# High parts of the gain-scaled transposed rows written by ScalarE instead of VectorE

## The chip, the cores and the metric

The kernel runs on one core of one Trainium2 chip. The metric is the device time of one execution in microseconds (us), the median of several. A profile of one further execution gives the trace that is read here. In views, PE is TensorE's matmul (PEld its weight load), ACT is ScalarE, DVE is VectorE, SP is SyncE, which issues nearly all DMAs.

## The reference

Two transformer blocks follow each other on 256 rows of width 2048, all in fp32. What matters here is that every block begins its stages with an RMS norm that has a weight vector `g`, and that the normed rows feed large matrix products:

```python
h = rmsnorm(x, g_mix)                       # 256 x 2048
proj = h @ w_in                             # then attention branches, gates
x = x + merged @ w_out
hm, mem_n = rmsnorm(x, g_mem_q), rmsnorm(mem, g_mem_kv)
x = x + mem_cross_attn(hm, mem_n, ...)
x = x + square(relu(rmsnorm(x, g_ff) @ w_ff1)) @ w_ff2
x = rmsnorm(x, g_final)                     # end of the first block
h = rms_norm(x, attn_norm);  x = x + hybrid_mixer(h, ...)
x = x + swiglu(rms_norm(x, ffn_norm), w_gate, w_up, w_down)
```

## The kernel before

A product of two fp32 matrices is done as three products of rounded parts (type fp32r): high x high, high x low, low x high. The weights come from HBM in groups of two k-tiles (128 x 1024 elements, 512 KB), through a ring of four buffers. For each group ScalarE writes the high part (`round_group`, L782) and VectorE the low part (`rest_to`, L1045); PE then runs 12 matmuls of 512 columns on it (L899 to L901), into two PSUM banks that belong to one 512-column chunk of the result.

The stationary side is the transposed rows, also in a high and a low part (`act_a_hi`, `act_a_lo`, `act_b_hi`, `act_b_lo`). A step "T" (a turn) makes two k-tiles of it: PE transposes four 128x128 blocks into one of the two auxiliary banks (L967) and raises `aux_done`; VectorE reads the bank and writes both parts (`turned`), and raises `aux_out`. The bank is free for the turn after the next, and the group that takes these tiles may start. Where the rows have still to be multiplied by a norm's weights (`"gain"` in the step), VectorE multiplies each half of the bank by a column of `gains` (L1241, two instructions of 256 columns) and then subtracts (L1245, two more). There are 50 such turns: 8 each for `g_mix`, `g_mem_kv`, `g_mem_q`, `g_ff`, `attn_norm_2` and `ffn_norm_2`, and 2 for `g_cq`. None of them is in a loop over repeated groups.

The order is written out by hand in `plan()`, as one list of steps; each engine walks the whole list and does its own part of each step, strictly in order. `weave` and `lead` put side steps between a chunk's groups. At step "G" number g, ScalarE rounds group g+3 (when its weights have landed and group g-1 is done) and VectorE does the low part of group g+2. Before the walk, ScalarE rounds the first three groups:

```python
for g in range(RING - 1):
    round_group(g, Turn())
```

The kernel then begins with `lead(cq, xt)`: turns 0 and 1, squares of the first rows (L838), group 0, turn 2, group 1, turn 3 and so on. SyncE loads weights and rows alternately: group 0, x part 0, group 1, x part 1, group 2, ... Before a group's load, SyncE waits until VectorE has done with the buffer (`lo_ready`).

Another place that is spoken of below is the start of the second block (around 1490 to 1550 us): there the steps "twice" (L1348, L1349) and "rstd" put much work on VectorE between the turns for `attn_norm_2`.

Of the kernel before, what the change touches and what calls it, by code (L numbers as in the profile page):

```python
# [32 lines left out]
ALU = mybir.AluOpType  # L33
ACT = mybir.ActivationFunctionType
AX = mybir.AxisListType

P = 128
SEQ = 256
# [39 lines left out]
G_ROWS = {"g_mix": 0, "g_mem_q": 16, "g_mem_kv": 32, "g_ff": 48, "attn_norm_2": 64, "ffn_norm_2": 80,  # L78
          "g_cq": 96, "fox_q_norm_2": 100, "fox_k_norm_2": 101, "nsa_q_norm_2": 102, "cmp_k_norm_2": 103,
          "slc_k_norm_2": 104, "win_k_norm_2": 105, "g_final": 106}  # L80
# [415 lines left out]
def two_blocks(nc, a, out):  # L496
    segments, groups = number(plan())
    ctx = ExitStack()
    with ctx:
# [3 lines left out]
        def sem(name):  # L503
            return ctx.enter_context(nc.semaphore(name))
# [22 lines left out]
        gains = sb("gains", [P, P])  # L527
# [56 lines left out]
        w_landed = [sem(f"w_landed{i}") for i in range(RING)]  # L584
        hi_ready, lo_ready, group_done = sem("hi_ready"), sem("lo_ready"), sem("group_done")
        chunk_out = [sem("chunk_out0"), sem("chunk_out1")]
        aux_done = sem("aux_done")
        aux_out = [sem("aux_out0"), sem("aux_out1")]
        rows_ready = sem("rows_ready")
        scores_done, row_max_ready, exp_done, probs_ready = map(sem, ("scores_done", "row_max_ready", "exp_done", "probs_ready"))  # L590
# [10 lines left out]
        def pt_of(unit, slot):  # L601

            return pt_sb[:, unit["u"] % 2 * 512:unit["u"] % 2 * 512 + 512] if unit["kind"] == "mem" else pt_sb[:, slot * 3 * P:(slot + 1) * 3 * P]

        def weights(c, i, turn):

# [158 lines left out]
        @block.scalar  # L765
        def _(act_e):
            act_e.dma_start(g_rows[0:KT, :], a["g_mix"].rearrange("a (k p) -> (a k) p", p=P)).then_inc(gmix_landed, 16)
            n, rstds, xs, sums = [0], [0], [0], [0]

            def step(ins):  # L770
                ins.then_inc(act_step, 1)
                n[0] += 1
                act_e.wait_ge(act_step, n[0])

            def round_group(g, turn):

                s, w = g % RING, groups[g]["width"]
                wait(act_e, w_landed[s], groups[g]["landed"], turn.landed)
                if g >= RING:

                    wait(act_e, group_done, g - RING + 1, turn.g)
                nc.scalar.activation(whi[:, s, 0:w], raw[:, s, 0:w], ACT.Copy).then_inc(hi_ready, 1)  # L782

            for g in range(RING - 1):
                round_group(g, Turn())

            def leave(c, turn):
                ev = c["ev"]
                if ev not in ("gate", "silu"):
                    return  # L790
                wait(act_e, group_done, c["end"], turn.g)
                wait(act_e, rstd_ready, rstds[0])
                if ev == "silu" and c["c"] >= 2:

                    wait(act_e, chunk_out[(c["c"] + 1) % 2], (c["c"] + 1) // 2, turn.c2)
                for t in range(NT):
                    src = prod_bank[c["c"] % 2 * 2 + t][:, :]
                    if ev == "gate":
                        ins = nc.scalar.activation(val[c["to"]][:, t, c["off"]:c["off"] + CH], src, ACT.Tanh, scale=s_("half_h", t, t + 1))
                    else:  # L800
                        ins = nc.scalar.activation(stage[:, 0, t, :], src, ACT.Silu, scale=s_("rstd_h", t, t + 1))
                ins.then_inc(chunk_out[c["c"] % 2], 1)

            def visit(kind, what, turn):
                if kind == "G":
                    if what["g"] + RING - 1 < len(groups):
                        round_group(what["g"] + RING - 1, turn)
                elif kind == "E":
                    leave(what, turn)
                elif kind == "gates":  # L810


                    act_e.wait_ge(forget_in, 1)
                    step(nc.scalar.activation(s_("e16"), s_("e16"), ACT.Exp, scale=-1.0))
                    nc.scalar.activation(s_("e16"), s_("e16"), ACT.Ln, bias=1.0).then_inc(forget_act, 1)
                    nc.scalar.activation(s_("gate"), s_("gate"), ACT.Tanh, scale=0.5).then_inc(gate_act, 1)
                elif kind == "rope":
                    act_e.wait_ge(angle_ready, 1)
                    nc.scalar.activation(s_("sin_in"), s_("sin_in"), ACT.Sin)
                    nc.scalar.activation(s_("red"), s_("red"), ACT.Sin).then_inc(sine_ready, 1)  # L820
                elif kind == "rstd":
                    rstds[0] += 1
                elif kind == "Q":
                    m = what["m"]
                    if what["of"] == "mem":
                        act_e.wait_ge(mem_landed, 16 * NT)
                    elif "r_fixed" in what["rows"]:
                        act_e.wait_ge(x_landed[m], 16)
                    else:
                        act_e.wait_ge(chunk_out[what["rows_c"] % 2], what["rows_c"] // 2 + 1)  # L830
                    if rstds[0]:

                        act_e.wait_ge(rstd_ready, rstds[0])
                    if sums[0]:

                        act_e.wait_ge(squared, sums[0])
                    for t in range(NT):
                        ins = nc.scalar.activation(act_junk[:, :], val[what["of"]][:, t, m * CH:(m + 1) * CH], ACT.Square,  # L838
                                                   accum_out=s_("ss", 4 * t + m, 4 * t + m + 1))
                        if t == 0:  # L840
                            step(ins)
                    ins.then_inc(squared, 1)
                    sums[0] += 1
                elif kind == "X":
                    x, j = xs[0], what["j"]
                    xs[0] += 1
                    act_e.wait_ge(aux_done, j + 1)
                    if x >= 2:
                        act_e.wait_ge(scored, x - 1)
                    nc.scalar.activation(rel[:, x % 2, :], aux_bank[j % 2][:, :], ACT.Relu).then_inc(aux_out[j % 2], 1)  # L850
                elif kind == "S":
                    u = what["u"]
                    act_e.wait_ge(row_max_ready, u + 1)
                    for t, (lo, hi) in enumerate(spans(what)):
                        v = s_sb[:, u % 2, lo:hi]
                        src = s_bank[u % 2][:, lo:hi] if what["kind"] == "mem" else v
                        total = None if what["kind"] == "cmp" else s_("rsum", u % 2 * 2 + t, u % 2 * 2 + t + 1)
                        ins = nc.scalar.activation(v, src, ACT.Exp, bias=s_("nmax", u % 2 * 2 + t, u % 2 * 2 + t + 1), scale=1.0, accum_out=total)  # L858
                    ins.then_inc(exp_done, 1)

            walk(act_e, visit, "act")


# [152 lines left out]

        @block.vector
        def _(dve):
            n, base, xs, rests, seen = [0], [0], [0], [0], [-1]
            v_e = nc.vector  # L1020

            def step(ins):

                ins.then_inc(dve_step, 1)
                n[0] += 1
                dve.wait_ge(dve_step, base[0] + n[0])
# [200 lines left out]
            def turned(what, turn):  # L1227
# [3 lines left out]
                if what["to"] in "AB":  # L1231
                    hi, lo = act[what["to"]]
                    cols = slice(k * SEQ, (k + 2) * SEQ)
                    if "gain" not in what:
                        step(v_e.tensor_copy(hi[:, cols], b[:, :]))  # L1235
                        v_e.tensor_tensor(lo[:, cols], b[:, :], hi[:, cols].bitcast(F32), ALU.subtract).then_inc(done, 1)
                        return
                    g0 = G_ROWS[what["gain"]] + (what["gain_k"] + what["col"] // P if "gain_k" in what else k)
                    for kk in range(2):
                        c1 = slice((k + kk) * SEQ, (k + kk + 1) * SEQ)  # L1240
                        ins = v_e.tensor_scalar(hi[:, c1], b[:, kk * SEQ:(kk + 1) * SEQ], gains[:, g0 + kk:g0 + kk + 1], None, ALU.mult)  # L1241
                    step(ins)
                    for kk in range(2):
                        c1 = slice((k + kk) * SEQ, (k + kk + 1) * SEQ)
                        ins = v_e.scalar_tensor_tensor(lo[:, c1], b[:, kk * SEQ:(kk + 1) * SEQ], gains[:, g0 + kk:g0 + kk + 1],  # L1245
                                                       hi[:, c1].bitcast(F32), ALU.mult, ALU.subtract)
                    ins.then_inc(done, 1)
                    return
# [260 lines left out]
```

## Time and profile before

| | us |
|---|---|
| median of 3 runs | 2705.02 (2704.07 to 2705.16) |
| the profiled execution | 2701.03 |
| its span, first to last instruction | 2699.3 |
| PE busy | 2657.9 (98%) |
| VectorE busy | 1785.9 (66%) |
| ScalarE busy | 1072.2 (40%) |

The span leaves 1.7 us of the profiled execution outside. A busy share is an average over stages. PE's share is modelled from pipelined matmuls; what PE isn't busy, 41.4 us, is the sum of its visible waits. The profiled execution lies 4 us below the median of the others, so differences are worked out against the trace and then added to the median.

### The profile page before, as it was taken

The page shows a single profiled execution, that of the slowest core. Times are in us where ns is not written, and L with a number is a line of the kernel's source. Part 1 is how long each engine was busy: PE and PEld are TensorE (multiplying, and loading weights), DVE is VectorE, ACT ScalarE, POOL GpSimd, SP SyncE. Part 2 cuts the span into 40 slices and gives each one's busy share as a digit, 9 for nine tenths or more (in the row PEclk, how much of TensorE's full clock was granted, in tenths as well). Part 3 has the DMA queues.
Part 4 walks back from the last instruction along what each step waited for, and adds up shares of the span by engine and source line. Part 5 has one row for each costly group of instructions (what it writes and reads, how often), then busy time and mean ns, then how long its engine had stood idle before and what let it go on. Part 6 is the DMA issues. An engine that isn't in the chain of part 4 may idle for free.

```text
span 2699.3 us, 33835 instructions
## 1 busy us (share of the span) xinstructions
PE 2657.9 (98%) x12280; PEld 2204.4 (82%) x12280; DVE 1785.9 (66%) x2651; ACT 1072.2 (40%) x1269; POOL 7.9 (0%) x43
## 2 busy tenths in 40 slices
PE   8999999999999999999999998999999999999998
PEld 7978888888878888888888777887888888888887
DVE  7678775576776656655665878898755555555555
ACT  4333344534343333333333433433343343444342
POOL 0000000000000000000000000000000000000000
PEclk9999999999999999999999998999999999999999
DMA  6545556555545555555555455444465555555554
GB/s 220 182 156 165 155 164 218 194 181 189 173 146 188 188 199 180 187 194 186 193 187 202 156 172 163 145 140 133 147 198 188 186 187 193 191 191 192 188 191 159
DMA packets 262080, 483.60 MB, mean 179 GB/s; under 512 B 17706, under 2 KB 38372, under 8 KB 261604
## 3 DMA queue, kind: packets, MB, share of 16 engines
q1 hardware_dynamic: 261956, 482.37, 54.6%
q8 instruction: 58, 0.95, 0.1%
q14 instruction: 34, 0.28, 0.0%
q10 hardware_dynamic: 32, 0.01, 0.0%
HBM read 480.22 MB, written 2.10 MB: 179 GB/s over the span
## 4 chain that ended last, share of the span: by engine, by line
PE 93%; DVE 5%; DMA 1%; issue 1%; ACT 0%; DVEq 0%; SPq 0%; ACTq 0%
PE bank L899 29%; PE bank L901 29%; PE bank L900 29%; PE bank L967 2%; DVE w_split L1045 2%; PE bank L930 1%; PE bank L998 1%; PE bank L983 1%; PE bank L1000 0%; PE bank L977 0%; DMA w_raw<-in_cmp_w_v 0%; PE bank L935 0%; DVE stage L1130 0%; DVE small L1072 0%; DVE scratch L1071 0%
## 5 line engine op out<-in xcount | busy, mean ns | idle before, releaser
L782 ACT ACTIVATE w_split<-w_raw 128x1024 fp32r<-128x1024 f32 (+2 forms) x920 | 959.9, 1046 | 1373.3 <-PE bank L901 1308.2
L1045 DVE TENSOR_TENSOR w_split<-w_raw,w_split 128x1024 fp32r<-128x1024 f32 (+2 forms) x920 | 1084.0, 1202 | 224.4 <-ACT w_split L782 221.9
L899 PE MATMUL bank<-w_split,act_a_hi 128*128 128x512 f32 (+2 forms) x2400 | 947.2, 395 | 10.1 <-DVE w_split L1045 9.1
L901 PE MATMUL bank<-w_split,act_a_lo 128*128 128x512 f32 (+2 forms) x2400 | 927.2, 386 | 0.0
L900 PE MATMUL bank<-w_split,act_a_hi 128*128 128x512 f32 (+2 forms) x2400 | 925.8, 386 | 0.0
L899 PEld LDWEIGHTS bank<-w_split,act_a_hi 128*128 128x128 f32 x2400 | 453.5, 189 | 97.6 <-DVE w_split L1045 7.1
L901 PEld LDWEIGHTS bank<-w_split,act_a_lo 128*128 128x128 f32 x2400 | 452.7, 189 | 89.2
L900 PEld LDWEIGHTS bank<-w_split,act_a_hi 128*128 128x128 f32 x2400 | 453.8, 189 | 82.9
L899 PE MATMUL bank<-w_split,act_b_hi 128*128 128x512 f32 x1248 | 490.8, 393 | 3.2 <-issue 2.9
L901 PE MATMUL bank<-w_split,act_b_lo 128*128 128x512 f32 x1248 | 486.3, 390 | 0.0
L900 PE MATMUL bank<-w_split,act_b_hi 128*128 128x512 f32 x1248 | 485.9, 389 | 0.0
L899 PEld LDWEIGHTS bank<-w_split,act_b_hi 128*128 128x128 f32 x1248 | 234.4, 188 | 53.5 <-issue 5.9
L901 PEld LDWEIGHTS bank<-w_split,act_b_lo 128*128 128x128 f32 x1248 | 234.2, 188 | 49.5
L900 PEld LDWEIGHTS bank<-w_split,act_b_hi 128*128 128x128 f32 x1248 | 234.5, 188 | 47.3
L1188 DVE TENSOR_TENSOR xres<-bank,xres 128x512 f32<-128x512 f32 x184 | 118.4, 685 | 185.6 <-PE bank L901 185.6
L1235 DVE CAST act_b_hi<-bank 128x512 fp32r<-128x512 f32 x54 | 37.3, 691 | 161.4 <-PE bank L967 161.4
L858 ACT ACTIVATE s_sb<-s_sb,small 128x128 f32<-128x128 f32 (+1 forms) x96 | 40.5, 431 | 169.6 <-DVE small L1288 169.6
L967 PE MATMUL bank<-ident,stage 128*128 128x128 f32 x386 | 57.7, 275 | 7.4 <-DVE stage L1078 6.9
L967 PEld LDWEIGHTS bank<-ident,stage 128*128 128x128 f32 x386 | 47.7, 141 | 19.5 <-issue 8.9
L1241 DVE TENSOR_SCALAR act_a_hi<-bank,gains 128x256 fp32r<-128x256 f32 x80 | 35.0, 478 | 27.2 <-PE bank L967 27.1
L1192 DVE TENSOR_SCALAR stage<-bank,small 128x512 f32<-128x512 f32 x32 | 22.5, 746 | 36.2 <-PE bank L901 36.2
L930 PE MATMUL bank<-heads 128*128 128x128 f32 (+2 forms) x208 | 43.2, 325 | 0.4 <-issue 0.4
(181 smaller groups left out, 926.0 us busy)
## 6 DMA issues: line engine op xcount, KB each, us to landing
w_raw<-in_w_ff SPq DMA_DIRECT2D x256, 512.0 KB, 4.4
w_raw<-in_w_in SPq DMA_DIRECT2D x208, 512.0 KB, 3.6
w_raw<-in_w_gate SPq DMA_DIRECT2D x88, 512.0 KB, 4.3
w_raw<-in_w_up SPq DMA_DIRECT2D x88, 512.0 KB, 4.6
w_raw<-in_w_down SPq DMA_DIRECT2D x88, 512.0 KB, 4.6
w_raw<-in_w_out SPq DMA_DIRECT2D x64, 512.0 KB, 4.0
w_raw<-in_w_in SPq DMA_DIRECT2D x24, 368.0 KB, 3.6
w_raw<-in_w_dsa_o SPq DMA_DIRECT2D x16, 512.0 KB, 4.8
```

Of the source, the lines that this page charges most:

```text
L782: nc.scalar.activation(whi[:, s, 0:w], raw[:, s, 0:w], ACT.Copy).then_inc(hi_ready, 1)
L858: ins = nc.scalar.activation(v, src, ACT.Exp, bias=s_("nmax", u % 2 * 2 + t, u % 2 * 2 + t + 1), scale=1.0, accum_out=total)
L899: pe.matmul(o, hi[:, cols], rhs_hi, start=k == 0, stop=False)
L900: pe.matmul(o, hi[:, cols], rhs_lo, start=False, stop=False)
L901: ins = pe.matmul(o, lo[:, cols], rhs_hi, start=False, stop=k == c["kt"] - 1)
L930: ins = pe.matmul(o, q[:, t * P:(t + 1) * P], k[:, 0:hi - lo], start=True, stop=not fox)
L967: ins = pe.transpose(b[:, kk * SEQ + t * P:kk * SEQ + (t + 1) * P], src[:, t, what["col"] + kk * P:what["col"] + (kk + 1) * P], ident[:, :])
L983: ins = pe.transpose(b[0:hi - lo, to:to + P], v[:, lo:hi], ident[:, :])
L1045: v_e.tensor_tensor(wlo[:, s, 0:w], raw[:, s, 0:w], whi[:, s, 0:w].bitcast(F32), ALU.subtract).then_inc(lo_ready, 1)
L1188: ins = v_e.tensor_tensor(x, b[t], x, ALU.add)
L1235: step(v_e.tensor_copy(hi[:, cols], b[:, :]))
L1241: ins = v_e.tensor_scalar(hi[:, c1], b[:, kk * SEQ:(kk + 1) * SEQ], gains[:, g0 + kk:g0 + kk + 1], None, ALU.mult)
```

## The change

ScalarE's walk now has a part for turns with a gain: it waits for the transposes (`aux_done`), multiplies both halves of the bank by their columns of `gains` into the high part, and raises a new semaphore, `turned_hi`. VectorE waits for that semaphore instead of multiplying, and then does only the subtraction. The first such step on ScalarE also waits until the first `gains` are written. Turns without a gain are as they were.

```diff
@@ -584,7 +584,7 @@
         w_landed = [sem(f"w_landed{i}") for i in range(RING)]
         hi_ready, lo_ready, group_done = sem("hi_ready"), sem("lo_ready"), sem("group_done")
         chunk_out = [sem("chunk_out0"), sem("chunk_out1")]
-        aux_done = sem("aux_done")
+        aux_done, turned_hi = sem("aux_done"), sem("turned_hi")
         aux_out = [sem("aux_out0"), sem("aux_out1")]
         rows_ready = sem("rows_ready")
         scores_done, row_max_ready, exp_done, probs_ready = map(sem, ("scores_done", "row_max_ready", "exp_done", "probs_ready"))
@@ -601,6 +601,9 @@
         def pt_of(unit, slot):
 
             return pt_sb[:, unit["u"] % 2 * 512:unit["u"] % 2 * 512 + 512] if unit["kind"] == "mem" else pt_sb[:, slot * 3 * P:(slot + 1) * 3 * P]
+
+        def gain_row(what):
+            return G_ROWS[what["gain"]] + (what["gain_k"] + what["col"] // P if "gain_k" in what else what["k"])
 
         def weights(c, i, turn):
 
@@ -765,7 +768,7 @@
         @block.scalar
         def _(act_e):
             act_e.dma_start(g_rows[0:KT, :], a["g_mix"].rearrange("a (k p) -> (a k) p", p=P)).then_inc(gmix_landed, 16)
-            n, rstds, xs, sums = [0], [0], [0], [0]
+            n, rstds, xs, sums, turns_hi = [0], [0], [0], [0], [0]
 
             def step(ins):
                 ins.then_inc(act_step, 1)
@@ -841,6 +844,17 @@
                             step(ins)
                     ins.then_inc(squared, 1)
                     sums[0] += 1
+                elif kind == "T" and "gain" in what:
+                    j, k = what["j"], what["k"]
+                    act_e.wait_ge(aux_done, j + 1)
+                    if turns_hi[0] == 0:
+                        act_e.wait_ge(aux_out[0], 1)
+                    for kk in range(2):
+                        g0 = gain_row(what) + kk
+                        ins = nc.scalar.activation(act[what["to"]][0][:, (k + kk) * SEQ:(k + kk + 1) * SEQ], aux_bank[j % 2][:, kk * SEQ:(kk + 1) * SEQ],
+                                                   ACT.Copy, scale=gains[:, g0:g0 + 1])
+                    ins.then_inc(turned_hi, 1)
+                    turns_hi[0] += 1
                 elif kind == "X":
                     x, j = xs[0], what["j"]
                     xs[0] += 1
@@ -1016,7 +1030,7 @@
 
         @block.vector
         def _(dve):
-            n, base, xs, rests, seen = [0], [0], [0], [0], [-1]
+            n, base, xs, rests, seen, turns_hi = [0], [0], [0], [0], [-1], [0]
             v_e = nc.vector
 
             def step(ins):
@@ -1235,11 +1249,9 @@
                         step(v_e.tensor_copy(hi[:, cols], b[:, :]))
                         v_e.tensor_tensor(lo[:, cols], b[:, :], hi[:, cols].bitcast(F32), ALU.subtract).then_inc(done, 1)
                         return
-                    g0 = G_ROWS[what["gain"]] + (what["gain_k"] + what["col"] // P if "gain_k" in what else k)
-                    for kk in range(2):
-                        c1 = slice((k + kk) * SEQ, (k + kk + 1) * SEQ)
-                        ins = v_e.tensor_scalar(hi[:, c1], b[:, kk * SEQ:(kk + 1) * SEQ], gains[:, g0 + kk:g0 + kk + 1], None, ALU.mult)
-                    step(ins)
+                    g0 = gain_row(what)
+                    turns_hi[0] += 1
+                    dve.wait_ge(turned_hi, turns_hi[0])
                     for kk in range(2):
                         c1 = slice((k + kk) * SEQ, (k + kk + 1) * SEQ)
                         ins = v_e.scalar_tensor_tensor(lo[:, c1], b[:, kk * SEQ:(kk + 1) * SEQ], gains[:, g0 + kk:g0 + kk + 1],
```

Line numbers move: L782 of before is L785 after, L838 is L841, L1045 is L1059, L1245 is L1257; the new multiplication is L854. PE's and SyncE's instructions keep their order.

What ScalarE's queue holds at the start of the kernel, before (w_split<-w_raw is the rounding of a weight group, act_junk the squares):

```order
L782 ACTIVATE w_split<-w_raw 128x1024 x3
L838 ACTIVATE act_junk,small<-xres 128x512 x2
L782 ACTIVATE w_split<-w_raw 128x1024 x2
L838 ACTIVATE act_junk,small<-xres 128x512 x2
L782 ACTIVATE w_split<-w_raw 128x1024 x2
```

and after:

```order
L785 ACTIVATE w_split<-w_raw 128x1024 x3
L854 ACTIVATE act_a_hi<-bank,gains 128x256 x4
L841 ACTIVATE act_junk,small<-xres 128x512 x2
L785 ACTIVATE w_split<-w_raw 128x1024
L854 ACTIVATE act_a_hi<-bank,gains 128x256 x2
L785 ACTIVATE w_split<-w_raw 128x1024
L854 ACTIVATE act_a_hi<-bank,gains 128x256 x2
```

The high parts of turns 0 and 1 now stand behind the roundings of the first three weight groups.

VectorE's queue at the same place, before:

```order
L1357 COPY gains<-bank 128x16
L1045 TENSOR_TENSOR w_split<-w_raw,w_split 128x1024
L1241 TENSOR_SCALAR act_a_hi<-bank,gains 128x256 x2
L1245 SCALAR_TENSOR_TENSOR act_a_lo<-bank,gains,act_a_hi 128x256 x2
L1241 TENSOR_SCALAR act_a_hi<-bank,gains 128x256 x2
L1245 SCALAR_TENSOR_TENSOR act_a_lo<-bank,gains,act_a_hi 128x256 x2
L1045 TENSOR_TENSOR w_split<-w_raw,w_split 128x1024
```

and after:

```order
L1369 COPY gains<-bank 128x16
L1059 TENSOR_TENSOR w_split<-w_raw,w_split 128x1024
L1257 SCALAR_TENSOR_TENSOR act_a_lo<-bank,gains,act_a_hi 128x256 x4
L1059 TENSOR_TENSOR w_split<-w_raw,w_split 128x1024
```

The two pairs of L1241 are gone and nothing else has moved, but the first L1257 now waits for ScalarE.

ScalarE's queue at the start of the second block, after; the four pairs of L854 are turns 4 to 7 for `attn_norm_2`. Before, the same rows stand there without L854:

```order
L785 ACTIVATE w_split<-w_raw 128x1024 x2
L854 ACTIVATE act_a_hi<-bank,gains 128x256 x2
L785 ACTIVATE w_split<-w_raw 128x1024 x2
L841 ACTIVATE act_junk,small<-xres 128x512 x2
L854 ACTIVATE act_a_hi<-bank,gains 128x256 x2
L785 ACTIVATE w_split<-w_raw 128x1024 x2
L854 ACTIVATE act_a_hi<-bank,gains 128x256 x2
L785 ACTIVATE w_split<-w_raw 128x1024 x2
L854 ACTIVATE act_a_hi<-bank,gains 128x256 x2
```

Each pair stands ahead of the rounding that follows its turn.

## Rows read from the trace of the kernel before

**Rows 1.** Busy time by stretch: us, PE, PEld, DVE, ACT, POOL, granted clock, DMA.

```profile
1480.00:1560.00 80.00, 74.62 (x342) 60.23 (x341) 69.78 (x140) 32.79 (x42) 2.85 (x12) 1.00 0.50 161
```

**Rows 2.** Waits: who <- whom, us in total, times, longest.

```profile
DVE act_a_hi L1241 <- PE bank L967: 27.1, 29, 3.5
DVE act_b_hi L1241 <- PE bank L967: 24.2, 10, 3.5
PE bank L899 <- DVE w_split L1045: 9.1, 8, 2.0
```

**Rows 3.** Groups by shape: busy us, mean ns of one, idle before.

```profile
L1241 DVE TENSOR_SCALAR act_a_hi<-bank,gains 128x256 fp32r<-128x256 f32 x80 | 35.0, 478 | 27.2 <-PE bank L967 27.1
L858 ACT ACTIVATE s_sb<-bank,small 128x256 f32<-128x256 f32 x8 | 3.7, 472 | 9.6 <-DVE small L1288 9.6
L799 ACT ACTIVATE heads<-bank,small 128x512 f32<-128x512 f32 x16 | 10.1, 684 | 13.9 <-PE bank L901 13.9
```

**Rows 4.** Order of time, start: start us, us, engine; merged when a count follows.

```profile
4.88 1.06 ACT L782 ACTIVATE w_split<-w_raw 128x1024 fp32r<-128x1024 f32 x1 [2.29 <-DMA w_raw<-in_w_in]
6.05 1.23 DVE L1045 TENSOR_TENSOR w_split<-w_raw,w_split 128x1024 fp32r<-128x1024 f32 x1 [1.58 <-ACT w_split L782]
8.04 0.88 DVE L1241 TENSOR_SCALAR act_a_hi<-bank,gains 128x256 fp32r<-128x256 f32 x2 [0.76 <-PE bank L967]
8.95 0.87 DVE L1245 SCALAR_TENSOR_TENSOR act_a_lo<-bank,gains,act_a_hi 128x256 fp32r<-128x256 f32 x2
9.88 0.80 PE L899 MATMUL bank<-w_split,act_a_hi 128*128 128x512 f32 x1 [1.02 <-DVE act_a_lo L1245]
11.10 1.06 ACT L782 ACTIVATE w_split<-w_raw 128x1024 fp32r<-128x1024 f32 x1 [1.65 <-DMA w_raw<-in_w_in]
12.06 0.62 ACT L838 ACTIVATE act_junk<-xres 128x512 f32<-128x512 f32 x1
15.90 0.88 DVE L1241 TENSOR_SCALAR act_a_hi<-bank,gains 128x256 fp32r<-128x256 f32 x2 [3.25 <-PE bank L967]
17.61 2.35 DVE L1045 TENSOR_TENSOR w_split<-w_raw,w_split 128x1024 fp32r<-128x1024 f32 x2
```

**Rows 5.** The chain that ended last, start: start us, us, what.

```profile
10.67 0.43 PE bank L900
...
15.37 0.50 PE bank L967 x4
15.86 0.23 PE bank L899
...
18.64 0.44 PE bank L967 x4
```

**Rows 6.** Order of time: PE, then ScalarE behind it; and a ScalarE pair of 512 columns.

```profile
217.09 1.13 PE L977 MATMUL bank<-misc,heads 64*128 64x256 f32 x4
...
218.25 0.60 ACT L850 ACTIVATE s_sb<-bank 128x512 f32<-128x512 f32 x1 [3.57 <-PE bank L977]
...
370.15 1.27 ACT L799 ACTIVATE heads<-bank,small 128x512 f32<-128x512 f32 x2 [2.63 <-PE bank L901]
```

**Rows 7.** Order of time, start of the second block: VectorE, then PE.

```profile
1512.35 0.87 DVE L1241 TENSOR_SCALAR act_a_hi<-bank,gains 128x256 fp32r<-128x256 f32 x2 [1.67 <-PE bank L967]
...
1518.16 2.35 DVE L1045 TENSOR_TENSOR w_split<-w_raw,w_split 128x1024 fp32r<-128x1024 f32 x2
...
1531.66 0.87 DVE L1241 TENSOR_SCALAR act_a_hi<-bank,gains 128x256 fp32r<-128x256 f32 x2 [0.30 <-PE bank L967]
...
1519.53 0.47 PE L899 MATMUL bank<-w_split,act_a_hi 128*128 128x512 f32 x1 [1.29 <-DVE w_split L1045]
...
1537.65 0.47 PE L899 MATMUL bank<-w_split,act_a_hi 128*128 128x512 f32 x1 [0.55 <-DVE w_split L1045]
1548.07 0.50 PE L899 MATMUL bank<-w_split,act_a_hi 128*128 128x512 f32 x1 [2.02 <-DVE w_split L1045]
```

## The prediction

> **What bounds the kernel now.** I read the busy times first, in the table above: PE is busy 2657.9 of 2699.3 us, VectorE for 66%, ScalarE for 40%. So of the whole span only 41.4 us are PE's waits, and time taken off VectorE is worth something only where PE stands still because VectorE is late. Next I asked for waits by name. VectorE's low parts of the weights hold PE up for 9.1 us in 8 places [rows 2]. Three of these 8 lie between 1480 and 1560 us, where PE is busy for 74.62 of 80 us and VectorE for 69.78 [rows 1]: 1.29, 0.55 and 2.02 us, at 1519.53, 1537.65 and 1548.07 [rows 7]. This is the only place where turns with a gain and PE's waits for VectorE lie together, and it holds 3.86 us.
>
> The same view says how the turns stand: before the multiplication VectorE had been idle, waiting for PE's transposes, in 29 + 10 = 39 of the 50 turns [rows 2]. There the turn is no backlog but a chain: transposes, high part, low part. In the other 11 VectorE came late, and only these can start their low part earlier when the high part moves away.
>
> Last I read the start in order of time. PE's first group waits for the low part of turn 0: multiplication at 8.04, subtraction at 8.95, first matmul at 9.88 [rows 4]. ScalarE rounds three weight groups there, as they land: the first at 4.88, the third not before 11.10, since its DMA ends then.
>
> **Removed.** 100 multiplications on VectorE at 478 ns [rows 3], two to a turn; a pair takes from 8.04 to 8.95, 0.91 us, until the subtraction starts [rows 4]. The 50 pairs are some 44 us of VectorE's 1786.
>
> **Added.** 100 multiplications on ScalarE, 256 columns out of PSUM with a column of numbers as scale. The trace has no such instruction, but it has near ones: 256 columns out of PSUM with a column as bias take 472 ns, and 512 columns out of PSUM with a column as scale 684 ns [rows 3]. A pair of the latter takes 1.27 us, so two overlap by 2 x 0.684 - 1.27 = 0.10 us [rows 6]. I take 2 x 0.472 - 0.10 = 0.84 us for a pair. It can't cost more than the pair of 512 columns, 1.27; the lower bound is one instruction alone, 0.47. ScalarE starts behind PE as quickly as VectorE does: 217.09 + 1.13 = 218.22, start at 218.25 [rows 6]. VectorE starts behind ScalarE 0.11 us later: 4.88 + 1.06 = 5.94, start at 6.05 [rows 4]. So where the transposes release the turn, the low part starts after 0.84 + 0.11 = 0.95 us instead of 0.91: +0.04 us. The turn gets no shorter; it only runs on two engines.
>
> The Trainium skill, ScalarE: Activation LUTs, section What ACT_TABLE_LOAD costs, gives 186 ns plus 0.833 ns a column, about 93 ns for each column operand, and 93 ns of overlap; an estimate from it is 2 x 492 - 93 = 891 ns for the pair. Its section Rules for kernel authors would leave multiplications on VectorE for speed; the rows here, 478 against 472 ns, show no such advantage for fp32 out of PSUM.
>
> **The start: the term that decides.** ScalarE walks in order, and the high part of turn 0 stands behind the rounding of the third weight group. After that rounding ScalarE took its next instruction at 12.06 [rows 4]; that slot now goes to turn 0. Its pair ends at 12.06 + 0.84 = 12.90, VectorE starts the low part at 13.01 and ends 0.87 later at 13.88, and PE starts 0.06 behind it, as 8.95 + 0.87 = 9.82 and 9.88 before: at 13.94. That is 13.94 - 9.88 = **+4.06 us**. Nothing of it hides: PE has nothing else to do there, it is busy without a gap from 9.88 on, and the waits later on are gated by PE and VectorE one behind the other, not by a fixed time. What VectorE does next shifts too: the low part of group 1 follows turn 1 and frees its buffer some 4 us later, so later loads start later by about what their consumers do. Turn 1's high part follows directly on ScalarE and is done before VectorE wants it.
>
> Then turn 2 is checked. Before, it starts at 15.90, and the low part of the weights of PE's third group, the first of the two at 17.61, ends at 17.61 + 1.18 = 18.8 [rows 4]; PE's transposes ahead of that group end at 18.64 + 0.44 = 19.1 [rows 5]. The 0.3 us between them cover the added 0.04, but not much more.
>
> **PE's pace.** The first group's matmuls of 512 columns follow each other every 0.43 us, from 9.88 to 15.37 [rows 4, 5], which is the 1.2 GHz level; afterwards every 0.23 us, and the second group takes 18.64 - 15.86 = 2.78 us [rows 5]. Before its first matmul PE had run transposes and then waited 1.0 us; now that wait is 5.1 us. If the slow stretch moves along unchanged the cost is 0. If the first group ran fast throughout, 5.49 - 2.78 = 2.7 us come back; if one more group runs slowly, 2.7 more are lost. I take 0 and keep both ends.
>
> **The second block's start.** VectorE's work without a pause before 1519.53 begins with turn 4, which the transposes release at 1512.35; that before 1537.65 and 1548.07 begins with turn 7, released at 1531.66 [rows 7]. Both turns are of the kind that gets 0.04 longer, so the three waits stay: 2 x 0.04 = +0.08 us. Turns 5 and 6 between them are late ones; their low parts start about 0.9 and 1.7 us earlier (one and two pairs of 0.87), and VectorE then waits for the transposes of turn 7 that much longer. ScalarE's roundings behind each turn start some 1.2 us later (transposes and pair), but they are for a group that PE reaches three groups, over 8 us, later, so PE doesn't see it. The other turns stand in stages in which PE doesn't wait for VectorE at all.
>
> **Sum.** 4.06 + 0.08 = +4.1 us: against the trace 2701.03 + 4.1 = 2705.2 with a span of 2703.4; on the median of the runs, 2705.02 + 4.14 = **2709.2 us**, 0.15% slower. About 0.2% (5.4 us) is what a measurement of this kernel tells from no change, so this most likely counts as none.
>
> **Rivals.**
> - *VectorE's relief reaches PE* (0.10). The 3.86 us of waits at the second block's start go away, because the late turns 5 and 6 pull all behind them forward. For it: VectorE is the busiest there relative to its time. Against it: VectorE idles again before turn 7 [rows 7]. It would give 4.06 - 3.86 = +0.2, 2705.3 us, not slower.
> - *All of VectorE's relief counts* (0.03). The 11 late turns give back 0.87 us each, 9.6 us, and the time is 2709.1 - 9.6 = 2699.5. Against it: that is more than the waits of PE that lie near them.
> - *A ScalarE pair is dearer than taken* (0.17). With the upper bound of 1.27 us, each released turn is 0.43 longer. Turn 0 pays it, turn 2 beyond its 0.3, turns 4 and 7 in full: 0.43 + 0.13 + 0.86 = +1.4 on top of the forecast, so 2710.6 us, slower than the bound. It decides from a pair of about 1.2 us on.
> - *The start isn't late* (0.03): the third weight group lands before the rows do in other executions, and ScalarE is free at 8. It would give 2705.1. Against it: SyncE issues that load behind the first rows.
>
> The forecast has 0.67 left. The estimate from the skill's page would put 0.05 on each of three turns, 2709.3 us.
>
> **Range.** The forecast with the pace term's ends is 2706.5 to 2711.9; the relief rival adds 2705.3 below, the dear pair lies inside. I give 2705.2 to 2712.0. Slower by over 0.2% means above 2710.4: the dear pair and a tenth of the forecast, where PE's pace loses over 1.2 us: 0.17 + 0.07 = 0.24; faster 0.03; the rest 0.73.
>
> **What would show it.** In the changed profile the first L899 should start at 13.9, released by the low part of turn 0, and the first L854 at 12.06. L854 should be about 470 ns. PE's waits for the low parts of the weights between 1480 and 1560 should still be near 3.9 us, all shifted by 4. VectorE should be busy 44 us less and ScalarE some 42 to 47 more, with VectorE's waits "for PE's transposes" turned into waits for ScalarE. I am wrong if PE starts before 12, or if PE waits at one of the other turns for a bank or a high part: then ScalarE's queue holds something up that I took for free.

## The result, and the profile after

| us | before | after |
|---|---|---|
| median, side by side on one chip | 2702.72 (20 runs) | 2706.84 (20 runs) |
| the profiled execution | 2701.03 | 2705.11 |
| its span | 2699.3 | 2703.4 |
| VectorE busy | 1785.9 | 1743.6 |
| ScalarE busy | 1072.2 | 1108.2 |

The ratio is 1.0015 with an interval of [1.0009, 1.0021]: 4.1 us slower, 0.15%, inside the bound under which it counts as no change, but a real loss: the interval excludes 1. The prediction was +4.1 us, 0.15%. As a time it was 2709.2, which is 2.4 us too high, because it was added to a median of three executions (2705.02), and the median of twenty is 2702.72. Of all executions on record two lie far off the others, one of before beside experiments 1 to 4 (4469.2 us, mean clock 0.556) and one of experiment 2 (3327.21 us, 0.753), and neither is in a ratio below.

The busy times at the head of the page, after:

```profile
PE 2657.8 (98%) x12280; PEld 2204.4 (82%) x12280; DVE 1743.6 (64%) x2551; ACT 1108.2 (41%) x1369; POOL 7.9 (0%) x43
```

PE is busy for the same time to 0.1 us while the span is 4.1 us longer: all of the loss is PE waiting. VectorE works 42.3 us less, and nothing of that reaches the end.

The start in order of time, after (start us, us, engine; merged where a count follows; idle before and releaser in brackets), to be read against [rows 4]:

```profile
11.16 1.06 ACT L785 ACTIVATE w_split<-w_raw 128x1024 fp32r<-128x1024 f32 x1 [1.64 <-DMA w_raw<-in_w_in]
12.13 1.55 ACT L854 ACTIVATE act_a_hi<-bank,gains 128x256 fp32r<-128x256 f32 x4
13.06 1.66 DVE L1257 SCALAR_TENSOR_TENSOR act_a_lo<-bank,gains,act_a_hi 128x256 fp32r<-128x256 f32 x4 [5.89 <-ACT act_a_hi L854]
13.99 0.79 PE L913 MATMUL bank<-w_split,act_a_hi 128*128 128x512 f32 x1 [4.85 <-DVE act_a_lo L1257]
...
20.05 0.84 ACT L854 ACTIVATE act_a_hi<-bank,gains 128x256 fp32r<-128x256 f32 x2 [4.06 <-PE bank L981]
```

Read it from below: PE's first group starts at 13.99 instead of 9.88, released by the low part; that starts at 13.06, released by ScalarE; ScalarE has no idle time before 12.13, where L854 follows directly on the third rounding, and that rounding waited 1.64 us for its weights. So a transfer which turn 0 doesn't need now stands ahead of it.

The chain that ended last, after, start of the kernel (start us, us, what), against [rows 5]:

```profile
14.78 0.43 PE bank L914
...
19.05 0.43 PE bank L915
19.47 0.54 PE bank L981 x4
20.02 0.23 PE bank L913
```

The first group runs at the slow pace from 13.99 to 19.47, 5.48 us; before from 9.88 to 15.37, 5.49 us. The slow stretch moved along whole.

The new instructions, and VectorE's, grouped by shape (count, busy us, mean ns of one, idle before), against [rows 3]:

```profile
L854 ACT ACTIVATE act_a_hi<-bank,gains 128x256 fp32r<-128x256 f32 x80 | 33.4, 471 | 46.7 <-PE bank L981 46.6
L1257 DVE SCALAR_TENSOR_TENSOR act_a_lo<-bank,gains,act_a_hi 128x256 fp32r<-128x256 f32 x80 | 34.9, 479 | 67.4 <-ACT act_a_hi L854 67.1
```

Waits after (who <- whom: us in total, times, longest), against [rows 2]:

```profile
DVE act_a_lo L1257 <- ACT act_a_hi L854: 67.1, 35, 5.9
DVE act_b_lo L1257 <- ACT act_b_hi L854: 33.4, 10, 4.5
PE bank L913 <- DVE w_split L1059: 9.2, 8, 2.0
PE bank L913 <- DVE act_a_lo L1257: 4.8, 1, 4.8
```

This is where the 42 us went. Before, VectorE idled 51.3 us ahead of 39 turns; now 100.5 us ahead of 45. What was taken off its work came back as waiting in the same chain, transposes, high part, low part. Most of it is nothing but ScalarE's time: 0.95 us from the transposes to the low part, 50 times, would be 47.5 us (an estimate from the prediction's 0.84 + 0.11). PE's waits for the weights' low parts are 9.2 us in 8 places against 9.1 in 8, untouched. What has grown is one wait, that at the start: 4.8 us where it was 1.0 [rows 4].

The second block's start (busy by stretch, columns as in [rows 1], its window moved on by 4 us), and then its turns 4 and 7 and PE's waits in order of time, against [rows 7]:

```profile
1484.00:1564.00 80.00, 74.53 (x341) 60.22 (x340) 62.76 (x124) 38.01 (x58) 3.03 (x13) 1.00 0.51 161
```

```profile
1516.64 0.84 ACT L854 ACTIVATE act_a_hi<-bank,gains 128x256 fp32r<-128x256 f32 x2 [2.04 <-PE bank L981]
1517.58 0.88 DVE L1257 SCALAR_TENSOR_TENSOR act_a_lo<-bank,gains,act_a_hi 128x256 fp32r<-128x256 f32 x2 [2.77 <-ACT act_a_hi L854]
1523.86 0.47 PE L913 MATMUL bank<-w_split,act_a_hi 128*128 128x512 f32 x1 [1.32 <-DVE w_split L1059]
1536.90 0.88 DVE L1257 SCALAR_TENSOR_TENSOR act_a_lo<-bank,gains,act_a_hi 128x256 fp32r<-128x256 f32 x2 [2.76 <-ACT act_a_hi L854]
1541.97 0.47 PE L913 MATMUL bank<-w_split,act_a_hi 128*128 128x512 f32 x1 [0.58 <-DVE w_split L1059]
1552.40 0.50 PE L913 MATMUL bank<-w_split,act_a_hi 128*128 128x512 f32 x1 [1.99 <-DVE w_split L1059]
```

VectorE is busy 62.76 instead of 69.78 of 80 us, and PE 74.53 instead of 74.62. Ahead of turn 7 VectorE idles 2.76 us, before 0.30 [rows 7]. Of the 2.46 us more, some 0.9 are ScalarE's pair, which now stands between the transposes and the low part; the other 1.5 are what VectorE gained at the late turns 5 and 6, and all of it is spent waiting for the transposes of turn 7. PE's three waits are 1.32, 0.58 and 1.99 against 1.29, 0.55 and 2.02.

### The profile page after: what moved, and what is told of

Its sections match the earlier page's. It is cut to its first block, busy times and chain, and to the rows that moved or that the text cites. A ratio compares the mean times of both kernels' runs of the same rounds, so it can differ in the third digit from the quotient of the medians.

```text
span 2703.4 us, 33885 instructions
## 1 busy us (share of the span) xinstructions
PE 2657.8 (98%) x12280; PEld 2204.4 (82%) x12280; DVE 1743.6 (64%) x2551; ACT 1108.2 (41%) x1369; POOL 7.9 (0%) x43
## 4 chain that ended last, share of the span: by engine, by line
PE 92%; DVE 6%; DMA 1%; issue 1%; ACT 0%; SPq 0%; DVEq 0%; ACTq 0%
PE bank L913 29%; PE bank L915 29%; PE bank L914 29%; PE bank L981 2%; DVE w_split L1059 2%; PE bank L944 1%; PE bank L1012 1%; PE bank L997 1%; PE bank L1014 0%; PE bank L991 0%; DMA w_raw<-in_cmp_w_v 0%; DMA w_raw<-in_w_in 0%; PE bank L949 0%; DVE stage L1144 0%; DVE small L1086 0%
## 5 line engine op out<-in xcount | busy, mean ns | idle before, releaser
L785 ACT ACTIVATE w_split<-w_raw 128x1024 fp32r<-128x1024 f32 (+2 forms) x920 | 959.7, 1046 | 1275.7 <-PE bank L915 1215.1
L1059 DVE TENSOR_TENSOR w_split<-w_raw,w_split 128x1024 fp32r<-128x1024 f32 (+2 forms) x920 | 1084.6, 1203 | 224.5 <-ACT w_split L785 222.0
L1257 DVE SCALAR_TENSOR_TENSOR act_a_lo<-bank,gains,act_a_hi 128x256 fp32r<-128x256 f32 x80 | 34.9, 479 | 67.4 <-ACT act_a_hi L854 67.1
L854 ACT ACTIVATE act_a_hi<-bank,gains 128x256 fp32r<-128x256 f32 x80 | 33.4, 471 | 46.7 <-PE bank L981 46.6
```

Of the source, the lines that this page charges most:

```text
L854: ins = nc.scalar.activation(act[what["to"]][0][:, (k + kk) * SEQ:(k + kk + 1) * SEQ], aux_bank[j % 2][:, kk * SEQ:(kk + 1) * SEQ], ACT.Co ...
L1059: v_e.tensor_tensor(wlo[:, s, 0:w], raw[:, s, 0:w], whi[:, s, 0:w].bitcast(F32), ALU.subtract).then_inc(lo_ready, 1)
```

## The experiments

Single executions of one and the same kernel differ by up to 4 us either way of their median (the last section shows where), so a difference of 1 to 4 us is read in two ways below: by the medians with their interval, and by a milestone, the start of the first transposes for the block that follows the eight `attn_norm_2` turns. In the traces of before, after and the experiments it moves by what happened ahead of it, and not by the scatter behind it. The ratios and intervals below are not exactly the quotients of the medians beside them (0.9988 in experiment 7, where the medians give 0.9980); where the two differ, the interval is what counts. The milestone:

```profile
1558.56 0.60 PE L967 MATMUL bank<-ident,stage 128*128 128x128 f32 x4
```

is before, and after it is 4.35 us later:

```profile
1562.91 0.60 PE L981 MATMUL bank<-ident,stage 128*128 128x128 f32 x4
```

The theory: the loss is ScalarE's order at the start and nothing else, and the 42 us taken off VectorE are worth nothing as the order stands. Rivals: the loss is spread over 50 turns, each of them dearer; or the relief does give something and the start costs more than it seems.

### 1 and 2: the first two turns apart from the other 48

In the first kernel turns 0 and 1 keep the multiplication on VectorE, and 48 turns are changed; in the second only turns 0 and 1 are changed. The condition of the first:

```diff
-                elif kind == "T" and "gain" in what:
+                elif kind == "T" and "gain" in what and (not (what["gain"] == "g_mix" and what["k"] < 4)):
...
-                    turns_hi[0] += 1
-                    dve.wait_ge(turned_hi, turns_hi[0])
+                    if not (what["gain"] == "g_mix" and what["k"] < 4):
+                        turns_hi[0] += 1
+                        dve.wait_ge(turned_hi, turns_hi[0])
+                    else:
+                        for kk in range(2):
+                            c1 = slice((k + kk) * SEQ, (k + kk + 1) * SEQ)
+                            ins = v_e.tensor_scalar(hi[:, c1], b[:, kk * SEQ:(kk + 1) * SEQ], gains[:, g0 + kk:g0 + kk + 1], None, ALU.mult)
+                        step(ins)
```

The second has the same without the "not".

> The changed kernel, but turns 0 and 1 keep their multiplication on VectorE; the other 48 are on ScalarE. Theory (the whole loss is the start: turn 0 stands behind ScalarE's third rounding): the first matmul comes back from 13.99 to about 9.9 us, the span from 2703.4 to 2699.4, equal to the kernel before, within 0.3 us. Rival (the 48 later turns hold something up too, or give something back): the span differs from 2699.3 by over 0.5 us; if VectorE's relief reached PE at the second block's start it would be down to about 2695.5.

Measured: 2701.28 against 2702.24 of before, ratio 1.0000 [0.9991, 1.0009]. The first matmul starts at 9.97, the milestone is at 1558.87, +0.31 on before:

```profile
1558.87 0.60 PE L981 MATMUL bank<-ident,stage 128*128 128x128 f32 x4
```

The expectation had named the span, and its one profiled span is 2702.8, which by the expectation's own sign speaks for the rival. Matching each matmul of PE with the same one of before settles it: the kernel is 0.2 to 0.4 us later up to the milestone, loses 1.6 us between the milestone and 1710, most of it from 1682 to 1686, and 1.6 more between 1861 and 1866, with PE at a slower pace both times (last section), and nothing lasting elsewhere. The milestone isn't wholly free of that either: between 1548 and 1552 eight matmuls ran at 0.43 us and cost 1.5 us, and PE's waits behind them shrank by nearly as much (4.2 us in 4 places instead of 5.4 in 5 from 1475 to 1570), so that nothing of it is left at the milestone.

> Only turns 0 and 1 are multiplied on ScalarE; the other 48 stay on VectorE as before. Theory: the whole loss is there, first matmul at 14.0, span 2703.3. Rival (the loss is spread over the turns): the span stays near 2699.5.

Measured: 2704.91 against 2702.24 of before, ratio 1.0015 [1.0006, 1.0024], the ratio of the whole change. The chain that ended last, start of this kernel:

```profile
12.66 0.37 ACT act_a_hi L854
...
13.13 0.89 DVE act_a_lo L1263 x2
...
14.06 0.80 PE bank L913
...
17.42 0.43 PE bank L914
17.85 0.28 PE bank L915
18.12 0.23 PE bank L913
```

PE starts at 14.06, 4.18 later than before, and the milestone is only +3.40:

```profile
1561.96 0.60 PE L981 MATMUL bank<-ident,stage 128*128 128x128 f32 x4
```

The difference is here: PE goes over to the 0.23 us pace at 17.85, after 8 matmuls at the slow one instead of 12. So 4 of the 100 moved multiplications, those of turns 0 and 1, carry the whole loss, the 96 others carry none, and the length of the slow stretch is worth 0.8 us between this execution and the others.

### 3 and 4: the same 50 turns on ScalarE, but fewer roundings ahead of turn 0

If it is the order, then an order in which turn 0 stands ahead of the third rounding must give the loss back, with all the work still on ScalarE. Two of the three first roundings stay ahead in the third kernel, one in the fourth; the rest follows turn 1:

```diff
-            for g in range(RING - 1):
+            for g in range(1):
...
                     turns_hi[0] += 1
+                    if turns_hi[0] == 2:
+                        for g in range(1, RING - 1):
+                            round_group(g, Turn())
```

(with 2 for 1 in both places in the third).

> The changed kernel, but ScalarE takes turns 0 and 1 behind the second rounding instead of the third. Theory: turn 0's high part starts 0.97 us after the second rounding's start at 8.4, at 9.4, the first matmul 1.88 later at 11.25, so the span is 2700.7. If the loss came of anything else than the place in ScalarE's queue (a slower hand-over, PE's pace after the longer wait), the span doesn't follow the place: 2703.

Measured: 2703.46 against 2702.24, ratio 1.0007 [0.9998, 1.0016]; milestone 1559.82, +1.26. The expectation had named a span of 2700.7, and 2703 if the span didn't follow the place; the profiled span is 2703.6. The start and the milestone follow the place, and the 3.1 us behind the milestone are lost at the same two places as in experiment 1 (last section). PE's first group:

```profile
11.25 0.79 PE L916 MATMUL bank<-w_split,act_a_hi 128*128 128x512 f32 x1 [2.29 <-DVE act_a_lo L1260]
```

> As the last, but only the first rounding stands ahead of turns 0 and 1; all 50 turns on ScalarE. Theory: turn 0 is released by PE's transposes at 8.0 again, first matmul 9.92, span 2699.4, the time of the kernel before. Rival: the second and third roundings, now 1 to 2 us later, hold up PE's second or third group or the loads behind them, and the span is 2700.5 or more.

Measured: 2702.16 against 2702.24, profiled span 2699.8 (2699.4 expected), ratio 1.0006 [0.9997, 1.0015]; milestone 1558.89, +0.33.

```profile
10.00 0.80 PE L916 MATMUL bank<-w_split,act_a_hi 128*128 128x512 f32 x1 [1.06 <-DVE act_a_lo L1260]
```

Three roundings ahead, two, one: PE starts at 13.99, 11.25, 10.00, and the milestone is 4.35, 1.26 and 0.33 us later than before. The size of the loss follows the number of roundings ahead of the turn. The fourth kernel's waits for the weights between 1475 and 1570 are the same as in before, 5.4 us in 5 places, so even with the start mended the relief gives nothing.

### 5: every pair of multiplications done twice

This asks what cover the turns have for a dearer pair. Each high part is written twice, with a wait for the first writing between (the value is the same):

```diff
-                    for kk in range(2):
-                        g0 = gain_row(what) + kk
+                    for again in range(2):
+                        if again:
+                            step(ins)
+                        for kk in range(2):
+                            g0 = gain_row(what) + kk
...
```

> The changed kernel with every high part written twice on ScalarE, the second pair behind the first: each turn on ScalarE takes about 0.9 us more, 45 us of ScalarE in all. Theory (only the chains that PE waits for count: turn 0 at the start, turn 2 beyond its 0.3 us of cover, turns 4 and 7 at the second block's start): first matmul at 14.9, and the span 0.9 + 0.6 + 0.9 + 0.9 = 3.3 us above the changed kernel's 2703.4, 2706.7. Rival 1 (every turn that the transposes release counts, 39 x 0.9): 2738. Rival 2 (ScalarE's share of the work doesn't matter beyond the start): 2704.3.

Measured: 2713.32 against 2702.91 of before, ratio 1.0041 [1.0028, 1.0055]; the profiled span is 2710.8, 7.4 over the changed kernel's, where the theory expected 3.3. The start was as expected, PE at 14.83. PE's waits for the low parts of the weights, first over the kernel, then from 790 to 840, where the turns for `g_ff` lie:

```profile
PE bank L916 <- DVE w_split L1062: 11.9, 12, 2.2
```

```profile
PE bank L916 <- DVE w_split L1062: 1.1, 2, 1.0
```

That is 11.9 us in 12 places instead of 9.2 in 8, and PE didn't wait from 790 to 840 in before. The second block's start in order of time:

```profile
1529.36 0.47 PE L916 MATMUL bank<-w_split,act_a_hi 128*128 128x512 f32 x1 [2.20 <-DVE w_split L1062]
...
1548.35 0.47 PE L916 MATMUL bank<-w_split,act_a_hi 128*128 128x512 f32 x1 [1.13 <-DVE w_split L1062]
```

These waits were 1.32 and 0.58 after, so turns 4 and 7 pay 0.9 and 0.55 in them. Where the 7.4 us lie shows when the same matmul is looked up in both traces (start in us; both have the same 12280 matmuls in the same order):

| the same matmul | after | experiment 5 | later by |
|---|---|---|---|
| the first | 13.99 | 14.83 | 0.8 |
| behind turn 2 | 23.15 | 24.66 | 1.5 |
| behind turn 6 | 35.97 | 37.96 | 2.0 |
| in the turns for `g_mem_q` | 706.93 | 708.95 | 2.0 |
| behind them | 727.60 | 730.31 | 2.7 |
| at the end of the turns for `g_ff` | 829.45 | 833.98 | 4.5 |
| ahead of turn 4's wait, second block | 1519.21 | 1523.84 | 4.6 |
| the milestone | 1562.91 | 1569.24 | 6.3 |
| the end of the span | 2703.4 | 2710.8 | 7.4 |

The expectation had four turns and 3.3 us. Turn 0 is 0.8 us, turn 2 is 0.7, turns 4 and 7 together are 1.7, so these came out as expected. It failed on the sum: it took them as the only turns without cover, and 3.1 us more were lost ahead of the milestone, 0.5 behind turn 6 at the start, 0.7 behind the turns for `g_mem_q`, 1.8 at those for `g_ff` and 0.1 on the way to the second block. The last 1.1 us lie behind the milestone, where executions of one kernel scatter too. So most other turns are covered against a second pair, and a few only in part. The rival that all released turns pay (39 times 0.9, 35 us) is far off.

### 6 and 7: an order in which the relief can count

If the relief is worth nothing only because VectorE waits for turn 7's transposes, then long VectorE work put ahead of the turns instead of behind them should let it count. "twice" piece 1 stood behind turn 4 and piece 3 behind turn 7; now each stands ahead:

```diff
-    seq += weave(down[3], [squares(1, down[1]), xt[2], squares(2, down[2]), xt[3]] + distances[4:6] + [xt[4], twice[1]], 1)
-    pend = [squares(3, down[3])] + [xt[5], distances[6], twice[2], xt[6], distances[7], xt[7], twice[3]]
+    seq += weave(down[3], [squares(1, down[1]), xt[2], squares(2, down[2]), xt[3]] + distances[4:6] + [twice[1], xt[4]], 1)
+    pend = [squares(3, down[3])] + [xt[5], distances[6], twice[2], xt[6], distances[7], twice[3], xt[7]]
```

The sixth kernel is the fourth with this order; the seventh is before with this order and nothing else.

> One rounding ahead of turns 0 and 1 as in the run before, all turns on ScalarE, and in the order of steps at the second block's start the two pieces of 'twice' now stand before turns 4 and 7 instead of behind them. Theory: the multiplication moved to ScalarE left VectorE idle for 2.8 us before each of these turns, and 'twice' (2.9 us) now fills it; PE's waits for low parts between 1480 and 1560 fall from 5.4 to about 1.6 us, span 2699.8 - 3.8 = 2696.0. Rival (VectorE is bound by its work there, wherever the idle time lies): the waits only move, 5 us of them stay, span 2699.4.

Measured: 2697.10 against 2702.91, ratio 0.9978 [0.9969, 0.9987], 5.8 us faster than before. The milestone, and PE's waits for the weights from 1475 to 1570:

```profile
1554.40 0.60 PE L984 MATMUL bank<-ident,stage 128*128 128x128 f32 x4
```

```profile
PE bank L916 <- DVE w_split L1062: 1.6, 2, 1.0
```

The milestone is 4.16 us earlier than in before, and 5.4 us of waits have become 1.6.

> The kernel before, with the same two pieces of 'twice' ahead of turns 4 and 7. VectorE's idle time before these turns is 1.67 and 0.30 us here, since it multiplies itself. Theory: about 1.5 us of PE's waits between 1480 and 1560 go, 3.9 stay, span 2699.3 - 1.5 = 2697.8; the difference to the kernel with the multiplication on ScalarE, 1.8 us or more, is what VectorE's relief is worth there once the order lets it through. Rival (the relief is worth nothing there): both reordered kernels have the same waits within 0.3 us.

Measured: 2697.38 against 2702.91, ratio 0.9988 [0.9979, 0.9997]. Its milestone and the waits of the same stretch:

```profile
1556.29 0.60 PE L967 MATMUL bank<-ident,stage 128*128 128x128 f32 x4
```

```profile
PE bank L899 <- DVE w_split L1045: 2.0, 3, 1.0
PE bank L899 <- DVE act_a_lo L1245: 1.5, 1, 1.5
```

The order alone gives 2.27 us at the milestone, with 3.5 us of waits left. The new one of them, 1.5 us, is for a turn's low part, VectorE being late with its own multiplication: just what the change takes off it. With the turns on ScalarE that wait is gone, and 1554.40 against 1556.29, 1.9 us, is what VectorE's relief is worth at the milestone once the order lets it through.

At the end it isn't shown. The medians are 0.3 us apart, the intervals overlap, and both profiled spans are 2695.2 us. The two traces, sixth kernel first, still have the 1.9 us at the next wait, and lose 1.5 of them within 5 us behind it:

```profile
1594.97 0.63 PE L984 MATMUL bank<-ident,stage 128*128 128x128 f32 x4 [3.12 <-DVE stage L1095]
1596.86 0.63 PE L967 MATMUL bank<-ident,stage 128*128 128x128 f32 x4 [3.12 <-DVE stage L1078]
```

```profile
1590.00:1605.00 15.00, 11.88 (x48) 9.40 (x47) 11.22 (x23) 3.46 (x4) 0.00 (x0) 0.89 0.54 159
1590.00:1605.00 15.00, 11.88 (x55) 9.61 (x54) 12.73 (x26) 4.24 (x4) 0.00 (x0) 1.00 0.63 188
```

In the sixth kernel PE goes back to 0.43 us a matmul behind this wait of 3.12 us, at a granted clock of 0.89, as in before (0.89 there too); in the seventh it doesn't. The same transposes at 1679.32 and 1679.19 have nothing of the lead left. Why the seventh kept its clock stays open, and so does what the relief is worth at the end.

### 8: only the eight turns that can count

Only the turns for `attn_norm_2` on ScalarE, with the order of the sixth; the start is that of before.

```diff
-                elif kind == "T" and "gain" in what:
+                elif kind == "T" and "gain" in what and (what["gain"] == "attn_norm_2"):
```

> The reordered start of the second block ('twice' ahead of turns 4 and 7), but only the eight turns for attn_norm_2 have their high part on ScalarE; the other 42, those at the kernel's start among them, stay on VectorE. Theory (VectorE's relief is worth something only at this one place): the same as with all 50 turns moved and one rounding ahead, PE's waits for low parts between 1480 and 1560 at 1.6 us, span 2695.2 within 1 us. Rival (relief in the other 42 turns is worth something too): the span is above 2697, and PE's waits elsewhere are longer.

Measured: 2697.16 against 2702.63, ratio 0.9983 [0.9974, 0.9992]; 1.5 us of waits in 2 places between 1475 and 1570, and the milestone

```profile
1554.18 0.60 PE L981 MATMUL bank<-ident,stage 128*128 128x128 f32 x4
```

0.2 us from the sixth kernel's, and the profiled span is 2694.9 where 2695.2 was expected. Eight turns do all that fifty do, as far as these runs tell, and the start needs no mending.

Not tried: handing over half a bank at a time, VectorE subtracting the first half while ScalarE multiplies the second. It would have two engines read one bank at once.

## Why the prediction was right, point by point

**The start, +4.06.** Right in mechanism and size: L854 at 12.13 (12.06 foretold), PE at 13.99 (13.94), +4.11. That the whole time came out at +4.1 to a tenth is partly luck: the interval runs from 2.4 to 5.7 us, the milestone is 4.35 later, and 0.3 us of that is given back behind it. As an absolute time, 2706.84 lies nearer to the 2705.3 of the rival in which the relief reaches PE than to 2709.2; what speaks against that rival is the difference, and the waits that are still there. Experiments 1 and 2 show that turns 0 and 1 alone carry the loss; 3 and 4 that the roundings ahead of them are its cause.

**The pair, 0.84 us.** Right: 471 ns for one, 0.84 for the pair, from near rows of other shapes. The rival of a dearer pair is out. It was priced on the turns 0, 2, 4 and 7 alone; experiment 5, with some 0.9 us more for each turn, lost 3.0 us at other turns too, so the price was probably low, but a pair of 1.27 us was not run. The estimate from the Trainium skill, ScalarE: Activation LUTs, section What ACT_TABLE_LOAD costs, was 492 ns for one and 891 ns for the pair; the trace is about 20 and 50 ns lower.

**The second block, +0.08.** The three waits named are 3.89 us after against 3.86 before [rows 7]; two steps of 0.04 can't be told apart from that. The milestone, 4.35 later where the start is 4.11 later, leaves 0.24 us for everything between, a little more than foretold.

**A count that was wrong.** The prediction said that three waits lie between 1480 and 1560, 3.86 us. The view of waits for that stretch of before has five, two more behind the three:

```profile
PE bank L899 <- DVE w_split L1045: 5.4, 5, 2.0
```

The reading in order of time had stopped at 1548, and the sum of the view wasn't used. The rival of a relief that reaches PE should have been priced with 5.4 us, 2703.8 instead of 2705.3, and the range's lower end would have been lower. The forecast didn't rest on it. Experiment 6, which removes 3.8 of those 5.4 us, shows that this wasn't an empty correction.

**The relief, 0.** Right, and for the reason given: VectorE idles before turn 7, and with the start mended (experiment 4) PE's waits there are still 5.4 us. The rival had a chance of 0.10, and experiments 6 and 7 show how little kept the relief from counting, the place of two steps in a list.

**PE's pace, 0.** Right in the profile, 5.48 against 5.49 us. Experiment 2 shows an execution in which it gives 0.8 us back, inside the ends that were kept.

**Busy times.** VectorE 42.3 us less (44 foretold). ScalarE 36.0 more where 42 to 47 were foretold: the L854 groups are busy for 33.4 + 8.4 = 41.8 us, but each pair's end overlaps the rounding behind it. After turn 4 the pair runs from 1516.64 for 0.84 and the rounding starts at 1517.37, 0.11 us of overlap; 50 of those would be 5.5 us, an estimate from this one.

## What to carry to other kernels

Work that is moved to a less busy engine takes the place in that engine's queue which its program gives it: look for what stands ahead of it there, above all prefetches that wait for a transfer, before counting what the old engine saves. An engine that idles before the moved work was part of a chain and not of a backlog, and its relief turns into waiting; it counts only at the places where the other engine's waits lead back to work without a pause, here 8 of 50 turns, and there only after two steps had changed places, with 1.9 us at the milestone. The 2697.2 us of the last kernel, 0.2% faster than before, are mostly the change of order: the order alone, with no multiplication moved, had 2697.4. Where a term rests on the waits of a stretch, let the view sum them, and don't read them off one by one.

## What was not expected of the hardware

The spans of one kernel scatter with the granted clock: among before's executions beside experiments 1 to 4 are one of 2696.3 us at a mean clock of 0.998 and one of 2704.4 at 0.993, about 1.6 us for each 0.001. Part of it sits in a stretch after the milestone in which PE waits often, and part around 1861. Busy times by stretch there, of before and of experiment 1 (granted clock third from the end):

```profile
1640.00:1680.00 40.00, 32.47 (x178) 30.36 (x177) 33.14 (x62) 16.05 (x18) 0.00 (x0) 0.84 0.62 181
1680.00:1720.00 40.00, 37.90 (x241) 35.74 (x239) 32.42 (x103) 17.54 (x40) 0.00 (x0) 0.99 0.45 133
```

```profile
1680.00:1720.00 40.00, 38.32 (x230) 36.27 (x229) 31.41 (x100) 17.11 (x38) 0.00 (x0) 0.94 0.46 127
```

The first two rows are before, the last is experiment 1: with a clock of 0.94 instead of 0.99 PE does 230 matmuls in the stretch instead of 241. The second place, before and then experiment 1:

```profile
1855.00:1870.00 15.00, 15.00 (x67) 10.73 (x66) 13.39 (x34) 5.12 (x15) 0.00 (x0) 1.00 0.33 107
1855.00:1870.00 15.00, 15.00 (x59) 10.60 (x58) 12.80 (x37) 3.98 (x10) 0.00 (x0) 0.89 0.35 108
```

PE is busy throughout in both, and does 59 matmuls instead of 67. In the traces of experiments 1, 2, 3 and 8 this second place costs 1.6 us, in the others nothing; the first costs 1.6 us in experiments 1 and 3 and gives as much back in 8. That accounts for the profiled spans of 1 and 3 that missed their expectation. Which execution meets a slower grant there, and why, stays open. For a change of a few us it means that one span isn't a measurement, and a milestone ahead of such places is a better one.
